# Moving the first block's final norm from the attention projection into the last input projections, with the reload of attention keys and the convolution projection shifted to make room

## What is computed

```
x = first_block(x, ...)        # ends with: return rms_norm(x, final_norm_g)
x = second_block(x, ...)

# in second_block
hx = modulate(rmsnorm(x, norm1_g), sh1, sc1)
q, k, v, u, b, c, g_attn, g_conv = split_projection(hx @ w_in)
q, k = axial rope of q, k
o_attn = latent_window_attention(q, k, v, k_ctx, v_ctx, sink)   # window 128 + 256 context keys
y_conv = b * conv3(c * u)
a = o_attn @ w_proj_attn ;  s = y_conv @ w_proj_conv
x = x + g1 * (sigmoid(g_attn) * a + sigmoid(g_conv) * s) @ w_out
x = x + g2 * expert_choice_moe(modulate(rmsnorm(x)), ...)       # 16 experts
return rmsnorm(x, final_norm_g)
```

## Time and profile before

| | |
|---|---|
| median of 3 runs | 2872.69 us (2872.62 to 2875.92) |
| the profiled execution | 2875.92 us, of which the profile's span is 2873.9 us |
| PE busy | 2748.8 us, 96% of the span |
| DVE / ACT / POOL busy | 2047.8 / 1306.1 / 550.0 us |
| end of the input projections on PE | 1698.5 us |
| attention with convolution projection | 1699.7 to 2046.5 us |
| attention projection | 2046.8 to about 2137 us |
| moved by DMA | 494.12 MB, mean 172 GB/s |

### The profile page before, as it was taken

The page is one execution under the profiler, slowest core; times in us unless marked ns, Lnnn a source line. Parts: engine busy times, 40 slices in busy tenths (PEclk is TensorE's granted clock), DMA queues, the critical chain, the costliest instruction groups (busy, mean ns, idle before and its releaser), DMA issues.

```text
span 2873.9 us, 35297 instructions
## 1 busy us (share of the span) xinstructions
PE 2748.8 (96%) x13692; PEld 2197.7 (76%) x13692; DVE 2047.8 (71%) x2927; ACT 1306.1 (45%) x2019; POOL 550.0 (19%) x491
## 2 busy tenths in 40 slices
PE   7999999999999999999999999999999399999997
PEld 6777778788778788988888876666778288888885
DVE  5344444888875587878877656766755689999997
ACT  4344433333323354443222344444323277777775
POOL 0011111655455010511111111111100300000000
PEclk9999999999999999999999999999999699999998
DMA  4110123344661997233222351111573689999996
GB/s 152 47 45 30 45 74 109 96 139 142 181 183 56 325 301 230 82 103 117 84 71 78 106 183 45 38 34 49 184 228 147 234 322 398 397 397 397 396 395 238
DMA packets 270554, 494.12 MB, mean 172 GB/s; under 512 B 30060, under 2 KB 141828, under 8 KB 269876
## 3 DMA queue, kind: packets, MB, share of 16 engines
q1 hardware_dynamic: 240800, 396.40, 39.6%
q0 software_dynamic: 29440, 95.43, 10.3%
q10 hardware_dynamic: 148, 0.04, 0.0%
HBM read 424.60 MB, written 67.21 MB: 171 GB/s over the span
## 4 chain that ended last, share of the span: by engine, by line
PE 85%; DVE 8%; DMA 3%; ACT 2%; issue 1%; POOL 1%; SPq 0%; POOLq 0%; DVEq 0%; ACTq 0%
PE PS L131 79%; PE PS L134 6%; DVE m L140 4%; ACT m L137 2%; DVE m L146 1%; DVE m L149 1%; DMA m<-in_w_down_dram 1%; DMA m<-x_scratch 1%; DVE m L182 0%; DVE m L185 0%; DVE m L179 0%; DMA x_scratch<-m 0%; DVE m L155 0%; ACT L137 0%; POOL m L140 0%
## 5 line engine op out<-in xcount | busy, mean ns | idle before, releaser
L131 PE MATMUL PS<-m,m 128*128 128x512 f32 (+6 forms) x11818 | 2553.8, 389 | 33.2 <-DVE m L140 17.9
L131 PEld LDWEIGHTS PS<-m,m 128*128 128x128 f32 (+2 forms) x11818 | 1986.3, 185 | 530.1 <-issue 113.7
L137 ACT ACTIVATE m<-m 128x512 fp32r<-128x512 f32 (+5 forms) x893 | 811.5, 929 | 910.5 <-DVE m L140 391.5
L140 DVE TENSOR_TENSOR m<-m,m 128x512 fp32r<-128x512 f32 (+4 forms) x928 | 1030.0, 1139 | 234.6 <-ACT m L137 212.2
L137 ACT ACTIVATE m<-PS 128x512 f32<-128x512 f32 (+3 forms) x481 | 268.7, 582 | 518.4 <-PE PS L134 331.9
L140 DVE TENSOR_TENSOR m<-PS,m 128x512 f32<-128x512 f32 (+1 forms) x456 | 300.4, 683 | 190.9 <-PE PS L131 147.3
L140 POOL TENSOR_TENSOR m<-m,m 128x512 f32<-128x512 f32 (+3 forms) x168 | 264.3, 1577 | 589.9 <-DVE m L140 262.7
L134 PE MATMUL PS<-ident,m 128*128 128x128 f32 x1650 | 229.9, 279 | 71.3 <-DVE m L155 36.0
L134 PEld LDWEIGHTS PS<-ident,m 128*128 128x128 f32 x1650 | 200.3, 144 | 106.1 <-DVE m L155 36.3
L149 DVE CUSTOM_DVE_ANT_0 m<-PS,m 128x640 f32<-128x640 f32 (+4 forms) x192 | 146.2, 774 | 86.9 <-PE PS L131 84.3
L155 DVE COPY m<-PS 128x512 f32<-128x512 f32 (+1 forms) x176 | 106.6, 614 | 125.0 <-PE PS L134 98.6
(11 more groups left out here) (88 smaller groups left out, 482.6 us busy)
## 6 DMA issues: line engine op xcount, KB each, us to landing
m<-in_w_exp_gate_dram SPq DMA_DIRECT2D x64, 1024.0 KB, 9.1
m<-in_w_exp_up_dram SPq DMA_DIRECT2D x64, 1024.0 KB, 9.3
m<-in_w_exp_down_dram SPq DMA_DIRECT2D x64, 1024.0 KB, 9.0
m<-in_w_mod_dram SPq DMA_DIRECT2D x48, 512.0 KB, 3.7
m<-in_w_gate_up_dram SPq DMA_DIRECT2D x44, 512.0 KB, 6.5
m<-in_w_in_dram SPq DMA_DIRECT2D x21, 1024.0 KB, 5.2
m<-in_w_in_dram SPq DMA_DIRECT2D x25, 512.0 KB, 5.2
x_scratch<-m POOLq DMA_DIRECT2D x24, 512.0 KB, 4.1
```

The costliest lines, as they stand in the source:

```text
L131: return Unsent() if self.e is None else self.e.matmul(o, l, r, start=first, stop=last, **k)
L137: return Unsent() if self.e is None else self.e.activation(o, i, fn, **k)
L140: return Unsent() if self.e is None else self.e.tensor_tensor(o, a, b, op)
```

## The change

1. `residual_norm` for the eight tiles is taken out of the attention projection and put into input groups 22, 23 and 24: tiles 0, 1, 2, then 3, 4, 5, then 6, 7. Loads and stores of the tiles move with it. Their buffers are now the ones that the convolution has just left (`yb[0]`, the region of `zb`, and the region of `ub` for the gain row).
2. The region of `ub` and `zb` is also where `k2` goes, so the load of `k2` now waits for the last `residual_norm` ("x2_last", 7) and stands on SP behind both `y_load`s instead of ahead of the convolution weights.
3. The first four parts of y are no longer split at the end of the input projections and the start of attention. All sixteen are split in steps 0 to 7, two per step.
4. Step 0 has no part of the convolution projection. Part p is done in step p+1 up to p = 57, parts 58 and 59 both in step 59, and parts 60 to 63 in their own steps as before. The first half of a part now stands before `values2` instead of behind it. `pc_take` and `pc_store` follow.
5. The waits that protected the old buffers move too (in the copy out of `turn2(0, 1)`, in `proj_act`).

Its core:

```diff
-        xr, growb = [piece(28, 1024, F32), piece(40, 1024, F32)], piece(24, 1024, F32)
+        xr, growb = [piece(44, 1024, F32), ar(152, 1024)], ar(148, 1024)
...
         def residual_load(sp, i):
             if i == 0:
-                sp.wait_ge("o2_acc", 15)
+                sp.wait_ge("zmul", 7, 1)
                 sp.dma_start(growb, final_norm_g.partition_broadcast(128)).then_inc(*sp.landed("grow_in"))
-            elif i >= 2:
+                sp.wait_ge("y_st0", 6)
+            elif i == 1:
+                sp.wait_ge("y_out", 7)
+            else:
                 sp.wait_ge(f"x2n_st{i % 2}", i - 2)
...
-            for c in range(2, NST):
+            for c in range(2, LAST):
                 w_load(sp, W_ST + c)
+            residual_load(sp, 0)
+            residual_load(sp, 1)
+            w_load(sp, W_ST + LAST)
+            residual_load(sp, 2)
...
+            residual_load(sp, 7)
             for n in range(18, 20):
                 sp.wait_ge(f"rope_st{n % 2}", n)
-            sp.wait_ge("zmul", 7, 1)
-            sp.wait_ge("y_st0", 6)
-            sp.wait_ge("y_st1", 7)
-            sp.dma_start(k2, ...).then_inc(*sp.landed("k_in"))
-            w_load(sp, W_PC)
-            w_load(sp, W_PC + 1)
             sp.wait_ge("st_acc", LAST, "P6")
             q_load(sp, 0)
+            sp.wait_ge("y_st0", 6)
             sp.wait_ge("st_acc", LAST, "P7")
             y_load(sp, 0)
             sp.wait_ge("st_acc", LAST, "P5")
             y_load(sp, 1)
+            sp.wait_ge("x2_last", 7)
+            sp.dma_start(k2, ...).then_inc(*sp.landed("k_in"))
             for i in range(1, 4):
                 q_load(sp, i)
...
+        FILL = {s: [s - 1] if s < 59 else [58, 59] if s == 59 else [s] for s in range(1, 64)}
+        FILL_END = {p // 4: s for s in FILL for p in FILL[s] if p % 4 == 3}
...
-            return [(n // 8, n % 8) for n in (2 * s + 4, 2 * s + 5)] if s < 6 else []
+            return [(n // 8, n % 8) for n in (2 * s, 2 * s + 1)] if s < 8 else []
...
                 if s + 1 < NS2:
                     qk2(pe, s + 1)
+                for p, k1 in halves[:len(halves) // 2]:
+                    fill_part(pe, p, k1)
                 if s and j == 0:
                     values2(pe, s // 4 - 1)
-                fill_part(pe, s, 0)
                 turn2(pe, s, 0)
                 turn2(pe, s, 1)
-                fill_part(pe, s, 1)
+                for p, k1 in halves[len(halves) // 2:]:
+                    fill_part(pe, p, k1)
...
-                if n < 8:
-                    residual_load(sp, n)
...
-                if 2 <= n < 10:
-                    residual_norm(dve, n - 2)
...
-            for i in range(NT):
-                residual_store(pool, i)
```

More of the change, by code:

```diff
@@ L2642, in second_sp @@
             y_load(sp, 1)
+            sp.wait_ge("x2_last", 7)
+            sp.dma_start(k2, q_dram[1024:1280, :].rearrange("(k p) n -> p k n", p=128)).then_inc(*sp.landed("k_in"))
             for i in range(1, 4):
@@ L2752, in second_act @@
                     gate_sigmoid(act, j, "21")
[L2753 to L2756, removed]
                     gate_sigmoid(act, j, "12")
@@ L2829, in second_dve @@
                 taps = [m for m in range(8) if C_AT["u", m] == c - 1]
+                resid = range(3 * (c - LAST + 2), min(8, 3 * (c - LAST + 3))) if c > LAST - 3 else ()
                 st_low(dve, c, "P3")
@@ L2838, in second_dve @@
                 st_low(dve, c + 1, "P6")
+                for i in resid[:1]:
+                    residual_norm(dve, i)
                 st_u3(dve, c)
@@ L2848, in second_dve @@
                 st_low(dve, c + 1, "P5")
+                for i in resid[1:2]:
+                    residual_norm(dve, i)
                 rope(dve, c, "11")
@@ L2854, in second_dve @@
                 rope(dve, c, "21")
+                for i in resid[2:3]:
+                    residual_norm(dve, i)
                 st_low(dve, c + 1, "P4")
-                if c == LAST:
-                    y_low(dve, 0, 0)
-                    y_low(dve, 0, 1)
                 st_c12(dve, c)
@@ L2885, in second_pool @@
                     zb_gate(pool, j, 1)
+                if c > LAST - 3:
+                    i = 3 * (c - LAST + 2)
+                    residual_store(pool, i)
+                    residual_store(pool, i + 1)
                 if kind == "g":
@@ L2891, in second_pool @@
                     gate_store(pool, j, 1, 0)
+                if LAST - 3 < c < LAST:
+                    residual_store(pool, i + 2)
+                if kind == "g":
                     gate_store(pool, j, 0, 1)
@@ L2907, in program @@
         yl_of = [rr(76, 8, 512), rr(92, 8, 512)]
-        yh_at = [64, 66, 124, 126, 108, 110, 112, 114, 116, 118, 120, 122, 68, 70, 72, 74]
-        yh = [rr(kb, 512) for kb in yh_at]
+        yh0, yh1a, yh1b = rr(108, 8, 512), rr(64, 6, 512), rr(124, 2, 512)
         gs = [ar(57, 512), ar(59, 512)]
@@ L3068, in mix_pe @@
                 j = s % 4
+                halves = [(p, k1) for p in FILL.get(s, []) for k1 in range(2)]
                 if s + 1 < NS2:
                     qk2(pe, s + 1)
+                for p, k1 in halves[:len(halves) // 2]:
+                    fill_part(pe, p, k1)
                 if s and j == 0:
                     values2(pe, s // 4 - 1)
-                fill_part(pe, s, 0)
                 turn2(pe, s, 0)
                 turn2(pe, s, 1)
-                fill_part(pe, s, 1)
+                for p, k1 in halves[len(halves) // 2:]:
+                    fill_part(pe, p, k1)
                 if len(chunks2(s)) == 3:
@@ L3089, in p2_evacuate @@
             if s == 0 and c == 1:
-                e.wait_ge("y_st0", 6)
+                e.wait_ge("x2n_st0", 6)
             if s >= 4:
@@ L3178, in mix_dve @@
             max2(dve, 0)
-            y_low(dve, 0, 2)
-            y_low(dve, 0, 3)
             for s in range(NS2):
@@ L3193, in mix_dve @@
                     o2_normed(dve, s // 4 - 1)
-                if s % 4 == 3:
-                    pc_take(dve, s // 4)
+                for n in range(16):
+                    if FILL_END[n] == s:
+                        pc_take(dve, n)
         def mix_masks(pool):
@@ L3212, in mix_pool @@
             for s in range(NS2):
+                for n in range(16):
+                    if FILL_END[n] == s:
+                        pc_store(pool, n)
                 if s % 4 == 3:
```

21 lines of the change are left out of this document (11 added, 10 removed).

## The result

The changed kernel takes 2893.65 us (median of 4 runs, 2892.61 to 2897.08) against 2872.95 us before: the ratio is 1.0073, with a 95% interval of 1.006 to 1.0085. It is slower by 20.7 us, not by the 7.4 us of the forecast, and outside the range. The profiled execution took 2895.7 us, of which 2893.6 us are the span.

A forecast was written before the change was run, and what follows sets the result against it. PE, busy 96% of the span, was taken as the bound. Start +8.5, input norms 0, first steps +1.2, moved part +1.6, projection -3.9 gave +7.4 us on the median 2872.69: about 2880 us, range 2873 to 2887.

The forecast's parts named there:

- part 5: Moved convolution projection parts: six matmuls go from step 0 to full step 59, +1.6 us; first half before values, 0.
- part 1: Attention projection: without norms, loads and stores there, PE's stop and the reduced clock after it go, 3.9 us gained.
- the stop of 2.20 us disappears: Attention projection: PE's stop at 2109.10 goes with the norm, 2.20 us of idle time plus 1.7 us of reduced clock.
- Part 2: Input projections: eight added norms, 10.2 us of DVE work, hidden by PE; one wait of 1 to 2 us; 0 us.
- Part 3: Start of attention: keys queued behind y land at 1709.4, first row maximum at 1710.7 instead of 1702.17, +8.5 us.
- part 4: First attention steps: four parts of y split ahead before now lie in the steps, +1.2 us, ends 0 and +4.
- at most 2.6 us go through: First attention steps: upper limit on how much of the extra y splitting on DVE reaches PE.
- a constant distance from step 8 to step 59: Sign in attention: from step 8 on, the distance to the kernel before stays constant until step 59.
- B: Rival: same mechanism but small, late start +5.8 us and extra y parts hidden; +3.5 us, 2876 us; chance 0.26.
- D: Rival: tiles come late in the input projections, two PE stops of some 3 us; 2886 us; chance 0.10.
- C: Rival: keys not held up by y at the start of attention; 2870.4 us, down to 2868.2 us; chance 0.08.

The follow-up runs named there:

- e3: Changed kernel with the first half of a step's fill behind the product with the values again; 2886.71 us, ratio 1.0045.
- e12: The kernel before, unchanged, profiled a second time; 2872.48 us, ratio 0.9995.
- e8: The kernel before with only the keys loaded behind both halves of y, no norm moved; 2879.27 us, ratio 1.0022.
- e9: The kernel before with only the convolution projection's parts one step later (58 and 59 together in step 59), still behind the values; 2878.60 us, ratio 1.0009.
- e10: The kernel before with only the first half of a step's fill put ahead of the values; 2903.25 us, ratio 1.0105.
- e13: Changed kernel with the values ahead of the fill again and y split two steps ahead; 2886.15 us, ratio 1.0037.
- e1: Changed kernel with the key load between the two halves of y instead of behind both; 2886.99 us, ratio 1.0045.
- e15: Changed kernel without loads, norms and stores of tiles 6 and 7, keys still behind both halves of y; 2890.04 us, ratio 1.0057.
- e6: Changed kernel with y splits, part schedule and PE's order of before; keys behind y, POOL's store still ahead of its product; 2885.03 us, ratio 1.0037.
- e2: Changed kernel with y split two steps ahead of its matmuls instead of one; 2892.23 us, ratio 1.0062.

## Why the prediction was wrong

The direction and the main mechanism of the start were right. The largest error is a term that the prediction put at nothing: part 5's "moves PE's order only, with PE full on both sides: 0" cost 5.8 us (e3). The gain of part 1 was not there, and the start was 2.5 us too small. Against the second profile of the kernel before, the trace of the changed one gives 11.8 us (first maximum) + 12.0 (attention) + 0.0 (projection) + 0.7 (rest) = 24.5, less 1.3 us by which E is earlier: 23.2 us, the difference of the spans 2893.6 and 2870.4. The forecast had 8.5, 2.8, -3.9 and 0. The medians differ by 20.7 us; the changed kernel's profiled execution was 2.1 us above its median.

**Part 1, the projection: -3.9 forecast, 0 found.** The failed step is "the stop of 2.20 us disappears" as a gain. It does disappear, but with its half clock it belonged to one execution: e12 and e8 are without it, and e9 and e10 have 1.15 and 0.25 us of it. The profiled execution was 3.2 us above the median of the runs, which the prediction noted as an offset and did not ask about. That was a hint, though a weak one: the profiled run of e13 was 4.0 us above its median and has no such stop.

**Part 2, the norms in the input projections: right.** PE has no gap there. Norm 6 waited 2.64 us for its load, somewhat more than the 1 to 2 us expected, and DVE had the room for it. Norms 0 to 5 waited at most 0.54 us, for instance in the changed kernel, DVE in order of time:

```profile
1658.21 1.28 DVE L146 SCALAR_TENSOR_TENSOR m<-m,small,m 128x1024 f32<-128x1024 f32 x1 [0.27 <-DMA m<-x_scratch]
...
1677.53 1.28 DVE L146 SCALAR_TENSOR_TENSOR m<-m,small,m 128x1024 f32<-128x1024 f32 x1 [0.54 <-DMA m<-x_scratch]
```

**Part 3, the start: +8.5 forecast, +11.0 found (+11.4 relative to E).** The mechanism was right and e8, e1 and e15 confirm it piece by piece: 7.2 to 7.5 us by the order, 4.3 to 4.5 by tiles 6 and 7. Two sizes were off. The landing of the second half of y was kept at 1704.05, although the loads of tiles 6 and 7 (issued from 1682.38 on) are in front of it and the stores of both beside it; it landed at 1689.89 + 18.3 = 1708.2. The prediction put 2.7 us for the two stores behind it instead, and the keys came only 2.6 us after it, so the two errors partly cancel by luck: the keys landed at 1710.8 instead of 1709.4. And the scores were priced at the 1.13 us of full clock, though a wait of ten microseconds was being predicted in front of them; at 1.2 GHz they took 2.08 us.

**Parts 4 and 5, the first steps and the moved part: +2.8 forecast, +12.0 found.** The experiments split the 12.0 us (differences of the unrounded values):

| step | attention | difference | what it is |
|---|---|---|---|
| changed to e3 | 356.4 to 350.7 | 5.8 | fill ahead of the values |
| e3 to e13 | 350.7 to 350.1 | 0.5 | y split one step ahead instead of two |
| e13 to e6 | 350.1 to 346.6 | 3.5 | four parts of y no longer split ahead of the loop, later parts, double step 59 |
| e6 to before (e12) | 346.6 to 344.5 | 2.1 | not in the schedule of PE or DVE, see below |

The first row was forecast as 0: in part 5 the values were not seen as cover. e3 shows what their place is worth here, e10 what it is worth where every tile border meets it (32.7 us). The second and third rows, 4.1 us, stand against the forecast's 1.2 + 1.6. Of these the double step 59 was right (1.4 us found in e9 and e13, 1.6 forecast). The failed step in part 4 is the limit "at most 2.6 us go through": it counted the work added to DVE, not the distance between a part's split and its use, nor the bank that DVE frees only behind the y parts (the stop of 2.34 us at step 5, e9). With a distance of one step PE, ACT and DVE form a ring. It is worth 2.5 us by itself (e2) but only 0.5 us once the values stand first (e13), so it is not the main part. In the changed kernel, pieces of one turn:

```profile
1722.26 1.03 PE L134 MATMUL PS<-ident,m 128*128 128x128 f32 x8
...
1722.89 0.60 ACT L137 ACTIVATE m<-PS 128x512 f32<-128x512 f32 x1 [1.76 <-PE PS L134]
...
1724.80 1.14 ACT L137 ACTIVATE m<-m 128x512 fp32r<-128x512 f32 x2
1725.45 1.29 DVE L140 TENSOR_TENSOR m<-m,m 128x512 fp32r<-128x512 f32 x2 [1.19 <-ACT m L137]
1726.19 0.96 PE L131 MATMUL PS<-m,m 128*128 128x512 f32 x3 [1.14 <-DVE m L140]
...
1726.99 1.03 PE L134 MATMUL PS<-ident,m 128*128 128x128 f32 x8
```

Transposes, ACT's copy (and two exponentials), high parts, low parts, matmuls, transposes: 1726.99 - 1722.26 = 4.73 us per step, against 3.5 to 4.4 before.

The last row has two parts, both read from the traces of e6 and e8 (the kernel before with only the keys late, 344.7 us). The transposes of step 0 begin 5.15 us after the first maximum in both, those of step 1 1.2 us later in e6 than in e8. In between the clock of e6 is still 0.50, until 1720, 8.0 us after its first maximum; in e8 it is back at 1714.7, 5.5 us after. The eight transposes of step 0 show it, first in e6, then in e8:

```profile
1717.13 1.91 PE L134 MATMUL PS<-ident,m 128*128 128x128 f32 x8
```

```profile
1714.36 1.22 PE L134 MATMUL PS<-ident,m 128*128 128x128 f32 x8
```

From there to the last step the distance stays the same within 0.1 us, and the other 0.8 us are the late product of POOL (see e9). The prediction had neither. The longer half clock and POOL's new order, item 4 of the change, cost 2 us between them.

The prediction also expected a constant distance from step 8 to step 59. It grew by 1.9 us there, all of it gone with the values first (e3).

**The rivals.** B to D fail. B's start was too small, and its extra parts of y did not hide. D did not occur: PE has no gap before 1698. C (keys not held up) is refuted by the landings: in the changed kernel, e1 and e8 the key load came back behind the y loads issued ahead of it each time.

## What to carry to other kernels

When work is moved between lists written out by hand, check for every producer how many steps lie between it and its use, and what stood between two uses of a bank: both are cover, and neither shows as busy time. A load put behind others in a full queue waited here for their whole backlog, including what the same change added ahead of them. The waits of 8.6 to 12.9 us were followed here by 8 to 10 us of half clock, which belongs into their price. And before a single stop in one profile is booked as a gain, look whether it is in a second profile.

## What was not expected of the hardware

With the fill between scores and values, the distance to the kernel before grew by about 0.15 us in every four steps, 1.9 us from step 8 to step 58, without a stop of PE; with the values first it did not. That order has one more change between tile shapes on PE in every fourth step, which is the likely reason, but no run separates it from the order itself. In the changed kernel PE was idle from 1698.02 to 1710.88, and the granted clock fell between 1703 and 1704. It stayed at 0.50 until 1720, although PE had begun again at 1710.88 and was idle again for 1.89 us ahead of 1714.85. In e8 it fell already between 1701 and 1702 and came back between 1714 and 1715, after a start at 1706.94. The stages that no edit touches moved the end of the input projections by up to 5.6 us between executions (1693.7 to 1699.3), more than most effects studied here.
